# GpSimd multiplies six rounds of hidden activations by their gates, in place of VectorE

## The reference

```
idx = jnp.take_along_axis(cand_idx, pos, axis=-1)
g = jax.nn.softmax(sc, axis=-1).astype(t.dtype)
...
act = jax.nn.gelu(jnp.einsum('thkd,td->thk', u[ib], tb), approximate=False)
return jnp.einsum('thk,thkd->td', gb * act, v[ib])
```

## Time and profile before

| | |
|---|---|
| time, median of 3 runs | 2995.97 us (2992.15 to 2996.62) |
| the profiled execution: its own time | 2992.3 us |
| the profiled execution: span from first to last instruction | 2990.2 us |
| PE, DVE, ACT, POOL busy in the span | 98%, 75%, 45%, 7% |
| granted TensorE clock | 0.998 of full speed |

### The profile page before, as it was taken

How to read it: one execution, slowest core, us unless ns; L and a number is a source line. 1 busy time by engine, 2 the same in 40 slices (tenths; PEclk the granted TensorE clock), 3 DMA queues, 4 the chain that set the end, 5 groups by cost and what they waited for, 6 DMA issues and landing times.

```text
span 2990.2 us, 48329 instructions
## 1 busy us (share of the span) xinstructions
PE 2933.8 (98%) x18854; PEld 2732.0 (91%) x18854; DVE 2252.9 (75%) x3250; ACT 1345.6 (45%) x1680; POOL 199.4 (7%) x225
## 2 busy tenths in 40 slices
PE   8999999999999999999999999999999999999998
PEld 8899879999999999999999999998888888888887
DVE  5777649996989999999999876898556656465564
ACT  4464343152445454545454555344454333333333
POOL 1000000001111111111111000000000000000000
PEclk9999999999999999999999999999999999999999
DMA  5443455589899999999999864544444555555554
GB/s 213 171 149 136 151 206 177 198 328 349 317 353 372 367 365 368 364 370 363 368 362 370 332 246 168 188 166 163 166 164 170 190 190 185 194 186 193 188 191 155
DMA packets 104915, 736.35 MB, mean 246 GB/s; under 512 B 12328, under 2 KB 12416, under 8 KB 17360
## 3 DMA queue, kind: packets, MB, share of 16 engines
q1 hardware_dynamic: 78272, 562.07, 51.3%
q0 software_dynamic: 24784, 159.91, 14.9%
q10 hardware_dynamic: 1728, 12.58, 1.0%
HBM read 717.12 MB, written 17.32 MB: 246 GB/s over the span
## 4 chain that ended last, share of the span: by engine, by line
PE 80%; DVE 12%; issue 3%; DMA 3%; ACT 2%; POOL 0%; SPq 0%; POOLq 0%; DVEq 0%; ACTq 0%
PE bank L2028 23%; PE bank L2029 11%; PE bank L2058 7%; PE bank L2059 7%; PE bank L2060 7%; PE bank L2006 5%; PE bank L2007 5%; PE bank L2008 5%; DVE split L1179 4%; PE bank L2355 4%; DVE set_rows L1654 2%; PE bank L2034 1%; DVE raw_lo L1179 1%; DVE got L1649 1%; DMA got<-u_rows_dram,row_idx 1%
## 5 line engine op out<-in xcount | busy, mean ns | idle before, releaser
L2028 PE MATMUL bank<-a_both,split 128*128 128x384 f32 (+1 forms) x3840 | 1177.8, 369 | 14.7 <-DVE split L1179 14.5
L1179 DVE TENSOR_TENSOR raw_lo<-raw,split 128x2048 fp32r<-128x2048 f32 x276 | 632.0, 2290 | 382.9 <-ACT split L739 379.9
L2028 PEld LDWEIGHTS bank<-a_both,split 128*128 128x128 f32 x3840 | 721.4, 188 | 67.7 <-issue 22.0
L739 ACT ACTIVATE split<-raw 128x2048 fp32r<-128x2048 f32 x276 | 527.8, 1913 | 497.4 <-DMA raw<-stream_dram 323.0
L2029 PE MATMUL bank<-a_both,split 128*128 128x192 f32 x3072 | 742.4, 252 | 0.0
L2029 PEld LDWEIGHTS bank<-a_both,split 128*128 128x128 f32 x3072 | 582.8, 191 | 0.0
L755 ACT ACTIVATE split<-raw 128x1536 fp32r<-128x1536 f32 x224 | 333.7, 1490 | 456.3 <-PE bank L2029 450.5
L1179 DVE TENSOR_TENSOR split<-raw,split 128x2048 fp32r<-128x2048 f32 x224 | 512.7, 2289 | 27.5 <-ACT split L761 12.3
L2006 PE MATMUL bank<-a_both,split 128*128 128x256 f32 x1472 | 425.1, 289 | 4.1 <-DVE a_both L1198 2.1
L2007 PE MATMUL bank<-a_both,split 128*128 128x256 f32 x1472 | 417.0, 283 | 0.0
L2008 PE MATMUL bank<-a_both,raw_lo 128*128 128x256 f32 x1472 | 417.0, 283 | 0.0
(11 more groups left out here) (344 smaller groups left out, 3332.1 us busy)
## 6 DMA issues: line engine op xcount, KB each, us to landing
raw<-stream_dram SPq DMA_DIRECT2D x532, 1024.0 KB, 4.9
gates_scratch<-stage ACTq DMA_DIRECT2D x12, 1024.0 KB, 9.1
gbuf<-gates_scratch POOLq DMA_DIRECT2D x30, 384.0 KB, 8.0
x<-x_dram SPq DMA_DIRECT2D x4, 512.0 KB, 6.8
x_scratch<-x POOLq DMA_DIRECT2D x1, 2048.0 KB, 11.1
mem<-mem_dram POOLq DMA_DIRECT2D x1, 2048.0 KB, 10.0
xm<-x_scratch POOLq DMA_DIRECT2D x1, 2048.0 KB, 12.3
out_dram<-x SPq DMA_DIRECT2D x4, 512.0 KB, 3.0
```

Source lines behind the costliest of these rows:

```text
L739: eng.activation(high(k, is_near(k))[:, :], raw[:, k % RAW, :], ACT.Copy).then_inc(hi_done, 1)
L1179: eng.tensor_tensor(low(k, is_near(k)), raw[:, k % RAW, :], high(k, is_near(k))[:, :].bitcast(F32), ALU.subtract).then_inc(split_done, 1)
L2028: mm(o, hi[:, ks], pair, start=kt == 0, stop=False)
```

## The change

In rounds 3 to 8 the multiplication of the GELU's 128 x 192 result by its gates is issued by POOL and no longer by DVE: 96 instructions. The waits in front of it (gates loaded, GELU done) and the signal behind it (`g_used`) go along. On POOL `gate_hidden(r, k)` stands at the head of unit k, before the reload of gates and before the gather that follows the unit's job. The first two rounds keep their gates on DVE.

```
@@ block.gpsimd
+            def gate_hidden(r, k):
+
+                g, j = k // 4, k % 4
+                if j == 0:
+                    eng.wait_ge(g_full[g], 16 * (r + (g >= 2)))
+                eng.wait_ge(tmp_full, BQ[f"u{r}"] + k + 1)
+                eng.tensor_tensor(blocks(tmp[:, j, 0:TD]), blocks(tmp[:, j, 0:TD]), gates_of(g, j), ALU.mult).then_inc(g_used, 1)
+
             for r in range(2, PEER_ROUNDS):
                 for kind in "ue":
                     for k in range(16):
+                        if kind == "u":
+                            gate_hidden(r, k)
                         if kind == "u" and k % 4 == 3 and r < PEER_ROUNDS - 1:
                             eng.wait_ge(g_used, 16 * r + k + 1)
                             load_gates(r + 1, k // 4)
@@ block.vector
-            def gate_hidden(r, k):
-
-                g, j = k // 4, k % 4
-                if j == 0:
-                    eng.wait_ge(g_full[g], 16 * (r + (g >= 2)))
-                eng.wait_ge(tmp_full, BQ[f"u{r}"] + k + 1)
-                weigh(tmp[:, j, 0:TD], g, j)
...
                     pair_add(r, k)
                     if k < 15:
                         ahead(UNIT0[f"u{r}"] + k)
-                    gate_hidden(r, k)
                     if k > 0:
                         act_lo(r, k - 1)
```

More of the change, by code:

```diff
@@ L548, in build, with gates_of, blocks @@
         block = ctx.enter_context(nc.Block())
+        def gates_of(slot, j):
+            return gbuf[:, bass.ds(slot, 1), :, j * TBLOCK:(j + 1) * TBLOCK].rearrange("p a b t -> p (a b) t")
+        def blocks(ap):
+            return ap.rearrange("p (b t) -> p b t", t=TBLOCK)
         @block.sync
@@ L1660, in _ @@
                     job(GROUP_JOBS[q])
[L1662 to L1667, removed]
             def weigh(tile, g, j):
```

## The result

| | before | after |
|---|---|---|
| median of 11 runs each, on one chip | 2996.62 us (2992.15 to 2998.06) | 3002.34 us (2998.88 to 3008.60) |
| ratio of the times, 95% interval | | 1.0023 (1.0015 to 1.0031) |
| span of the profiled execution | 2990.2 us | 2998.2 us |

The changed kernel is slower by 0.23%, 6.9 us (4.5 to 9.3). The forecast was 3003.6 us, 0.25% slower.

What follows compares the result with a forecast made beforehand. PE was taken to set the up stages' pace, with DVE close behind. +6.6 (gates holding DVE) + 0 (unit 15) + 1.0 (load of `mem`) = +7.6 us, so 2995.97 becomes 3003.6 us; range 2990 to 3014.

Steps and rivals of the forecast that it cites:

- What bounds the kernel: Up stages: PE sets the pace, DVE close behind; a DVE change d per unit changes six stages by 30d.
- Who is next: At the shared SBUF read port after DVE's subtraction: longest waiter first, so POOL reads while DVE stands; 0.58 with h up to 0.57.
- DVE keeps its queue going: Rival: DVE's next instruction takes the port, POOL runs only at `pair_add`; -6.4 to -4.1 us with `mem`, about 2990.5; chance 0.28.
- the load of `mem` alone decides: Rival: gates cost DVE what they did before (h = 0.27), leaving 0 to 1.5 us in round 8; no separate chance.
- The hold h: Time DVE stands while POOL's gate reads through the port, behind the subtraction: taken as 0.49 us.
- all passes overlap: Low end for h: the gate's input and output passes over 192 elements run together, giving 0.31 us.
- two inputs in turn: Chosen case for h: the gate's two inputs are read one after the other, giving 0.49 us.
- d: Change of DVE's time per up unit, h - 0.27: forecast 0.22 us, so +6.6 us over six up stages.
- DVE becomes the bound: Rival: with h over about 0.57 DVE sets the up stages' length; 3007 to 3014 us; chance 0.14.
- The gates' length: Sign: POOL's 96 gates last about 2.5 us each, waiting included, ending about 0.5 after a subtraction.
- The load of `mem`: End of round 8: issued behind unit 15's gate, the load lands late and PE waits 0 to 1.5 us; taken as +1.0.
- Unit 15, gathers, reloads: Unit 15's later gate costs 0, at most 0.2 us per stage; gathers and reloads queued behind gates cost nothing.

Runs made afterwards that it cites:

- no gate: The changed kernel with POOL's 96 multiplications left out and their waits and signal kept; 2989.46 us, ratio 0.9981 to the kernel before.
- half gate: The changed kernel with POOL multiplying only 96 of the 192 columns of each gate tile; 2993.49 us in one run, kernel before 2996.16.
- mem early: The changed kernel with the load of `mem` issued ahead of round 8's last four gates; 2999.69 us against 2995.96 for the kernel before, ratio 1.0011.
- two gates: The changed kernel with a second multiplication of the same size into spare memory ahead of each gate; 3015.83 us in one run, kernel before 2996.16.
- mem late only: The kernel before, gates on DVE, with the load of `mem` issued behind round 8's last gate; 3000.40 us against 2995.96, ratio 1.0014.
- gate at pair_add: The changed kernel with `mem` loaded early and POOL's gates (units under 15) held until ACT copied the next unit's bank; 2989.91 us against 2995.96, ratio 0.9979.

## Why the prediction was right, and where its sizes were off

- **What bounds the kernel** held. A place of two jobs costs PE twice what a DVE unit grows by. Change of DVE's unit with a job against change of the six up stages: -0.27 and -7.5 us (no gate), -0.07 and -2.2 (half gate), +0.13 and +3.5 (changed kernel), some 27 to 31 us for 1 us, where the prediction had 30.
- **Who is next** was the step that decided, and it was chosen right: the waiting POOL instruction goes ahead of DVE's next. The rival that DVE keeps its queue going is out: its unit with a job would have been 5.2, and is 5.58. The rival that the load of `mem` alone decides is out by mem early, which keeps the long up stages.
- **The hold h was too large**: 0.49 forecast, 0.40 measured. The reasoning by passes put it between 0.31 and 0.67, and the measured one lies between "all passes overlap" and "two inputs in turn". With it d is 0.13 and not 0.22, and the up stages grow by 3.5 and not by 6.6. The same error gave the unit of 5.65 (5.58). PE's unit 9 was put at 5.9 and takes 5.58, for a second reason as well: the prediction laid the whole growth on unit 9, and half of it fell on unit 8 (4.71 to 4.86). A single up stage grew by 0.6, not 1.1.
- **DVE becomes the bound** did not happen; two gates shows that it would at twice the hold.
- **The gates' length**, 2.5 forecast, is 2.02 on the mean: in a unit that follows one with a job the gate's start lies behind a gather of 0.98, which the prediction did not count; in such a unit the gate lasts some 1.9. Their end, 0.45 behind the subtraction, is as forecast (0.5).
- **The load of `mem` was too cheap**: 1.0 forecast, at most 1.5; 2.7 measured. The issue came where it was expected, 2.0 us behind the end of the up stage (1.9). The step that failed is the landing: it was put at 7.5 to 10.0, "since the gathers beside it are over", and it took 11.1 (9.5 to 11.1 in the six kernels that load late, 10.8 in mem late only). So the copy and the subtraction behind the square came 3.6 later against the end of the up stage, not 2.4. By the prediction's own chain that makes a PE wait of 2.7 instead of 1.5. The row of the wait is 2.33: the chain let PE react some 0.4 behind the subtraction, which no row shows, and PE started 0.05 behind it. The unit itself then took 0.27 more than the 4.55 of before, and the stage is 2.7 longer.
- **Unit 15, gathers, reloads**: nothing of theirs shows. The five down stages, forecast at 0, are +0.5.

So the total is near for a partly lucky reason: the gates are 3.1 under and the load 1.7 over, two errors against each other, and +0.5 in the down stages was not forecast. The three sum to +6.7, inside the timed 4.5 to 9.3.

The -1.5 behind the last down stage is TensorE's clock. These are the same 3.4 us of the second block's cross attention, before and after (bounds, then busy us by engine, granted clock, DMA):

```profile
2217.50:2220.90 3.40, 3.40 (x16) 3.16 (x15) 2.07 (x1) 2.58 (x2) 0.40 (x2) 0.50 0.03 5
```

```profile
2227.00:2230.40 3.40, 3.40 (x29) 3.32 (x28) 2.08 (x1) 2.58 (x2) 0.39 (x2) 1.00 0.03 7
```

In both PE had just waited 2.05 us for ACT's `cqT`. Before, the granted clock then stood at its lower level for 3.4 us, PE got 16 matmuls in and not 29, and the 1.5 us are lost there. The same fall is in the trace of mem late only, and in none of the other seven. **Open** is why: the seven are those whose DVE has 96 instructions fewer, but one trace of each kernel cannot say whether that has a part in it.

## What to carry to other kernels

Moving a small two-input operation from VectorE to GpSimd does not take it off VectorE where VectorE's neighbours read two SBUF tiles: here 0.27 us a unit went and 0.40 came back as a stall of the next instruction, which shows in the length of an instruction that was not touched. Before such a move, look for a VectorE instruction with one SBUF input to lay it beside; with the load early in both, holding the gate back until `pair_add` turned +0.11% into -0.21%. And list what an in-order queue holds behind the new instruction: one late load cost 2.7 us, the 96 multiplications 3.5.

## What the runs showed of the hardware that was not expected

- **A gather's issue is held by a subtraction too.** The gather at 932.63 above, 0.14 ahead of the subtraction, took 0.98; that of gate at pair_add at 937.32, 0.19 into one, took 2.95 and ended 0.85 behind the subtraction's end. In that kernel all 48 gathers that started inside a subtraction ended 0.81 to 0.89 behind its end, and the other 80 took at most 1.15. An indirect DMA takes its indices from an SBUF tile (`row_idx`); that it is the reading of them that waits is not shown. In the kernel before only 4 gathers started inside a subtraction, of which one is here (POOL, then DVE):

```profile
902.56 2.59 POOL L651 DMA_INDIRECT got<-u_rows_dram,row_idx  x1 [0.30 <-issue]
...
902.04 2.29 DVE L1179 TENSOR_TENSOR split<-raw,split 128x2048 fp32r<-128x2048 f32 x1 [0.17 <-ACT split L761]
```

- **The turns.** With two POOL operations one behind the other (two gates), DVE and POOL alternated instruction by instruction: subtraction, first gate, `act_lo`, second gate, job. Neither engine ran its queue out.
